# Loads of the first experts' weights cut in halves, and the table of slot weights built behind the first down product

## The chip, the cores and the metric

The kernel runs on 1 core of one Trainium2 chip. The metric is the device time of one execution in microseconds (us). Every expert weight is read from device memory once per execution.

## The reference

Two layers, each a mixer (eight heads of softmax attention with a forgetting bias, four heads of retention, an output projection) and then a mixture of 32 experts on 512 tokens of width 1024, two experts chosen for each token. All arithmetic is float32.

```python
for layer in range(2):
    x = x + mixer(rmsnorm(x, norm_mix_w[layer]), w_in[layer], fox_forget_b[layer], w_out[layer])
    x = x + hierarchical_moe(rmsnorm(x, norm_ffn_w[layer]), ...)
return rmsnorm(x, norm_final_w)

def hierarchical_moe(h, ...):
    # a softmax over 4 groups picks the group, top 2 of its 8 experts are taken, weights = group * pair
    ...
    def expert_block(args):
        xblk, e = args
        a = jax.nn.silu(xblk @ w_expert_gate[e]) * (xblk @ w_expert_up[e])
        return a @ w_expert_down[e]
    ...
    out = jax.ops.segment_sum(yb * w_buf[:, None], tok_buf, num_segments=N)
```

Gate and up are 1024 x 512 and down is 512 x 1024 for each expert, so each of the three is 2 MiB (2.10 MB) and an expert is 6.29 MB.

## The kernel before

**A layer** is a written-out list of steps for the mixer, the output projection, the router and the dispatch tables, and then a loop over the 32 experts. The list ends with the output projection ("wo"): for each of four token tiles and each half of the columns, eight chunks `c` of the contraction, three matmuls a chunk (L1715 to L1717). The second column half of tile 3 is the last; between its matmuls stand transposes, router logits and the ranks of chosen tokens. Then come four gathers by matmul of the first two experts' tokens (L1756), and the loop over experts.

**An expert** has 64 slots. TensorE does for expert `e`: gate (32 matmuls of 64 x 256, L1834) and up (32 more), then transposes of the hidden rows (L1843), for the middle experts the input transposes of the next expert (L1800), then down (16 matmuls, L1850). The result of expert `e - 1` is added to the tokens by one-hot matmuls, the "spread" (L1808): tiles 0 and 1 after gate and up of `e`, tiles 2 and 3 after its down. ScalarE makes the silu (L1016) and the scaled high part of the result (L1020). VectorE makes the product of gate and up (L1429), copies the transposed hidden rows (L1451), prepares the next input (L1415, L1426), the one-hot of the slots (L1438), the low part of the result (L1433), and adds the spread to the residual (L1170).

**The first experts** carry work for the tables besides. In expert 0 TensorE makes behind gate and up the table of tokens by slot (`slots_by_expert`, L1535) and the table of slot weights (`weights_by_expert`, L1542, eight float32 products that the profile counts as 16), then the transposes, then down. VectorE reads the token table (L1086, L1087), makes the product, copies the table of slot weights (`slot_weights`, L1102), which ScalarE's scaling waits for, copies the hidden rows, takes the input of expert 1, makes the one-hot, and then runs `further` (L1183 to L1207, 20 small operations for the tokens beyond 64 of an expert); only after that comes the low part of expert 0's result (L1433), for which the spread in expert 1 waits. `further` also gives the one-hots for a table that TensorE makes behind gate and up of expert 1 (L1535), and a weight table behind those of expert 2 (L1542).

**The loads** of expert weights are issued by SyncE (the SP queue), in order, into a ring of three expert-sized places. Each place is also used by the mixer: what is not yet read bars the load. So the order is: up of 0 after the last input projection; gate, up and down of 1 after the retention; gate of 0 and gate of 2 when the first column half of the output projection is done; down of 0, up of 2 and down of 2 when the second is done. From then on `load_expert` waits for gate, up and down of expert `e - 3` one after the other (semaphores `s_gh`, `s_gu`, `s_yf`) and loads the same matrix of `e` each time. GpSimd stores the normalized rows of each token tile (4 stores of 512 KB a layer) and gathers the rows of experts 2 and up with indirect DMAs (L760), through its own queue.

`down_rows` gives each of the 128 partitions two pieces of two rows each (8 KB each), and gate and up give it 8 consecutive rows, 16 KB.

Of the kernel before, what the change touches and what calls it, by code (L numbers as in the profile page):

```python
# [14 lines left out]
P = 128  # L15
DEPTH, T, D = 2, 512, 1024
NT = T // P
KC = D // P
# [4 lines left out]
NE = NG * EPG  # L23
# [3 lines left out]
NEG = -3.0e38  # L27

SLOTS = 64
N_SMALL = 6 * DEPTH + 2 * (DEPTH - 1)  # L30

MAXBLK = T // SLOTS
NOV = max(k for k in range(NE * MAXBLK)
# [7 lines left out]
EXPERT = 2 * KC * DE + (DE // P) * D  # L41
RING = 3
TAIL = NE % RING or RING
SLAB = KC * P
HT0 = 0
KT0 = HT0 + 2 * KC * T
# [252 lines left out]
def trunk_kernel(nc, x, norm_mix_w, w_in, fox_forget_b, w_out, norm_ffn_w, w_router_group, b_router_group,  # L299
                 w_router_expert, b_router_expert, w_expert_gate, w_expert_up, w_expert_down, norm_final_w,  # L300
                 const, rope, decay, number, out):
    with ExitStack() as ctx:
# [3 lines left out]
        def sem(name):  # L306
            return ctx.enter_context(nc.semaphore(name))
# [138 lines left out]
        s_tokn = sem("token_numbers_loaded")  # L446
# [111 lines left out]
        def _(sp):  # L558
# [42 lines left out]
            def down_rows(layer, e):  # L601

                return w_expert_down[layer, bass.ds(e, 1), :, :].rearrange("a (b p j) n -> p (a b) (j n)", b=2, p=P)

            def load_rows(layer, e, slot, i):

                weight = (w_expert_gate, w_expert_up)[i]
                sp.dma_start(wexp[slot][0][:, i, :, :].rearrange("p c n -> p (c n)"),
                             weight[layer, e, :, :].rearrange("(p c) n -> p (c n)", p=P)).then_inc(s_w[slot][i], 16)
# [3 lines left out]
                    load_rows(layer, e, slot, i)  # L613

            def load_down(layer, e, slot):
                sp.dma_start(wexp[slot][1].rearrange("p (b j) n -> p b (j n)", b=2), down_rows(layer, e)
                             ).then_inc(s_w[slot][2], 16)

            for layer in range(DEPTH):
                if layer == 0:  # L620
                    load_x(0)
                    load_slab(layer, 0)
                    load_x(2)
                    load_slab(layer, 1)
                    sp.dma_start(kst[:, P:NCONST], const[:, P:NCONST]).then_inc(s_const, 16)
                    sp.dma_start(tokn[:, :], number).then_inc(s_tokn, 16)
                load_slab(layer, RAW)
                if layer > 0:
                    sp.wait_ge(s_yf, layer * NE)
# [29 lines left out]
                load_rows(layer, 2, 2, 0)  # L659


                is_full(sp, ("wo", 3, 1), layer)
                load_down(layer, 0, 0)
                load_rows(layer, 2, 2, 1)
                load_down(layer, 2, 2)

                def load_expert(e, slot):

                    for i, used in enumerate((s_gh, s_gu)):
                        sp.wait_ge(used, e + (layer * NE - RING + 1))  # L670
                        load_rows(layer, e, slot, i)
                    sp.wait_ge(s_yf, e + (layer * NE - RING + 1))
                    load_down(layer, e, slot)

                for e in range(RING, NE):
                    load_expert(e, e % RING)
# [377 lines left out]
        def _(dve):  # L1054
# [154 lines left out]
            for layer in range(DEPTH):  # L1209
# [230 lines left out]
                def hidden(e):  # L1440
                    g = layer * NE + e + 1
                    if e == NE - 1:
                        for t in range(2):
                            add_spread(layer, e - 1, t)
                    dve.wait_ge(s_sg, g)
                    dve.wait_ge(s_gu, g)
                    gated_product().then_inc(s_h, 1)
                    if e == 0:
                        slot_weights(layer)
                    dve.wait_ge(s_hxf, g)  # L1450
                    nc.vector.tensor_copy(at(HX0, 256), bank[2][:, 0:256]).then_inc(s_hx, 1)  # L1451
                    if e < NE - 1:
                        take_input(e + 1)
                    if e == 0:
                        is_taken(dve, ("table",), layer)
                    slot_one_hot(e, slot_tok[:, e:e + 1]).then_inc(s_oh, 1)
                    if e == 0:
                        further(layer)
                    if e and e < NE - 1:
                        for t in range(2):  # L1460
                            add_spread(layer, e - 1, t)
# [12 lines left out]
                take_input(0)  # L1474
                route(layer)
                if layer == 0:
                    dve.wait_ge(s_tokn, 16)
# [47 lines left out]
        def _(pe):  # L1525
# [50 lines left out]
            for layer in range(DEPTH):  # L1576
                srow = layer * FH * NT
                for s in STEPS_OF[layer]:
# [126 lines left out]
                    elif kind in ("begin", "wp", "wo"):  # L1705
# [3 lines left out]
                        for c in chunks[kind] if kind != "wp" else range(2 * s[3], 2 * s[3] + 2):  # L1709
                            if t == 0:  # L1710
                                pe.wait_ge(s_ml, layer * KC + c + 1)
                                pe.wait_ge(s_wol, layer * KC + 4 * half + c // 2 + 1)
                            m_hi, m_lo = (m[:, c, P * t:P * (t + 1)] for m in (mix_hi, mix_lo))
                            w_h, w_l = wo_hi[half][:, c, :], wo_lo[half][:, c, :]
                            mm(o[:, :], m_hi, w_h, start=(c == 0), stop=False)  # L1715
                            mm(o[:, :], m_hi, w_l, start=False, stop=False)  # L1716
                            last = mm(o[:, :], m_lo, w_h, start=False, stop=(c == KC - 1))  # L1717
                    elif kind == "fT":
                        t, half = s[1], s[2]
                        is_taken(pe, ("wo", t, half), layer)  # L1720
# [103 lines left out]
                def gate_up(slot, before=None, parts=False):  # L1824

                    w = wexp[slot][0]
                    for i in range(2):
                        if before is not None:
                            before(i)
                        for c in range(KC):  # L1830
                            if parts and i == 0 and c == 4:
                                pe.wait_ge(s_xt, input_part(layer, 0))
                            for half in range(2):
                                last = mm(bank[i][SLOTS * half:SLOTS * (half + 1), 0:256],  # L1834
                                          xT[:, c % 4, c // 4, :], w[:, i, c, 256 * half:256 * (half + 1)],
                                          start=(c == 0), stop=(c == KC - 1))
                        if before is not None and i == 0:
                            last.then_inc(s_gh, 1)
                    return last
# [6 lines left out]
                def down(slot, into=3):  # L1846
# [7 lines left out]
                def per(i):  # L1854
                    return len(range(i, NE, RING))

                def expert(e):
                    i, g = e % RING, layer * NE + e + 1
                    loads = 16 * (layer * per(i) + e // RING + 1)
                    pe.wait_ge(s_xt, input_part(layer, e) - (e == 0))  # L1860

                    def ahead(part):
                        if part and e == NE - 1:
                            spread_block(e - 1, (0, 1))
                        pe.wait_ge(s_w[i][part], loads)

                    gate_up(i, ahead, e == 0).then_inc(s_gu, 1)
# [16 lines left out]
                    pe.wait_ge(s_w[i][2], loads)  # L1884
                    down(i).then_inc(s_yf, 1)
                    if e and e < NE - 1:
                        spread_block(e - 1, (2, 3))

                first_transpose()
                for e in range(NE):  # L1890
                    if e == 1:
                        for name in (("count",), ("table",), ("wtab",)):
                            is_taken(pe, name, layer)
                        may_fill(pe, ("more",), layer)
                    expert(e)

                o = ov[layer]
# [60 lines left out]
```

## Time and profile before

| | |
|---|---|
| time, median of 3 executions | 1526.78 us (1525.1 to 1527.63) |
| the profiled execution's own time | 1525.63 us |
| its span, first to last instruction | 1523.8 us |
| TensorE matmul busy | 1478.5 us (97%) |
| VectorE / ScalarE / GpSimd busy | 829.1 / 369.7 / 259.7 us |
| mean granted TensorE clock | 0.996 of full |
| DMA moved, mean | 463.84 MB, 304 GB/s |
| loop over experts, layer 0 | about 299.5 to 757 us |
| loop over experts, layer 1 | about 1050 to 1510 us |

Times of rows are us from the span's start. A matmul's busy time overlaps that of the next one, so the starts say more than the busy sums. The time from a DMA's issue to its landing contains the time that it stands behind earlier DMAs of its queue.

### The profile page before, as it was taken

Reading aid. Unit: us, or ns where it says so; the run is one execution under the profiler, and the core shown is the slowest. Engines: PE = TensorE matmul, PEld = TensorE weight load, DVE = VectorE, ACT = ScalarE, POOL = GpSimd, SP = SyncE. Lnnn points to the kernel's source line nnn. Section 1 sums busy time; section 2 is a strip of 40 time slices with the busy share of each in tenths; the row PEclk is TensorE's granted clock in tenths of the full one; section 3 lists DMA queues with packets and bytes.
Section 4 is the critical chain, followed back from the end, with each engine's and each line's share of the span. In section 5 each row is a group of like instructions: output and inputs, shape, how many; then the busy total and the mean of one; then the engine's idle time right before and its main releaser. Section 6 shows DMA issues by size and latency. Waiting matters only on the chain.

```text
span 1523.8 us, 23589 instructions
## 1 busy us (share of the span) xinstructions
PE 1478.5 (97%) x9360; PEld 929.8 (61%) x9360; DVE 829.1 (54%) x1602; ACT 369.7 (24%) x726; POOL 259.7 (17%) x155
## 2 busy tenths in 40 slices
PE   8999999999999999989999999999999999999996
PEld 6877768655555555545588777685555555554453
DVE  2267763655555455454525686636555545554546
ACT  6335464400000000000163354732000000000002
POOL 3342332110000000000134331401000000000001
PEclk9999999999999999999999999999999999999998
DMA  6442146599999999999833321478999999999995
GB/s 220 93 98 69 42 166 275 226 417 420 424 421 425 420 424 422 424 422 425 328 111 84 85 69 28 172 289 321 416 422 421 425 422 421 422 425 422 424 424 213
DMA packets 105616, 463.84 MB, mean 304 GB/s; under 512 B 16515, under 2 KB 59779, under 8 KB 72481
## 3 DMA queue, kind: packets, MB, share of 16 engines
q1 hardware_dynamic: 98208, 449.14, 73.7%
q0 software_dynamic: 5952, 12.09, 2.1%
q8 instruction: 78, 1.28, 0.3%
q10 hardware_dynamic: 1344, 1.05, 0.2%
q14 instruction: 34, 0.27, 0.1%
HBM read 463.81 MB, written 6.29 MB: 308 GB/s over the span
## 4 chain that ended last, share of the span: by engine, by line
PE 80%; DMA 17%; DVE 2%; issue 1%; DVEq 0%; ACTq 0%
PE bank L1834 23%; DMA area<-in_w_expert_up_dram 16%; PE bank L1850 11%; PE bank L1808 7%; PE bank L1645 5%; PE bank L1650 5%; PE bank L1649 5%; PE bank L1715 2%; PE bank L1717 2%; PE bank L1571 2%; PE bank L1716 2%; PE bank L1573 2%; PE bank L1572 2%; PE bank L1665 2%; PE bank L1687 1%; DVE area L1451 1%
## 5 line engine op out<-in xcount | busy, mean ns | idle before, releaser
L1834 PE MATMUL bank<-area 128*64 128x256 f32 x4096 | 459.8, 381 | 15.7 <-DMA area<-in_w_expert_up_dram 14.5
L1834 PEld LDWEIGHTS bank<-area 128*64 128x64 f32 x4096 | 287.5, 137 | 182.5 <-issue 24.3
L1170 DVE TENSOR_TENSOR xres<-xres,bank 128x512 f32<-128x512 f32 x512 | 316.2, 679 | 5.0 <-PE bank L1808 5.0
L1850 PE MATMUL bank<-area 128*64 128x512 f32 x1024 | 235.0, 601 | 7.5 <-DVE area L1451 2.2
L760 POOL DMA_INDIRECT area<-rows,gath x60 | 68.0, 1133 | 725.1 <-PE bank L1800 702.7
L1020 ACT ACTIVATE y_hi<-bank,slot_w 128x512 fp32r<-128x512 f32 x64 | 44.0, 688 | 580.3 <-PE bank L1850 580.3
L726 POOL TENSOR_TENSOR w_lo<-area,w_hi 128x1024 fp32r<-128x1024 f32 x55 | 135.2, 2459 | 272.7 <-ACT w_hi L833 272.6
L1429 DVE TENSOR_TENSOR area<-area,bank 128x256 f32<-128x256 f32 x64 | 26.9, 421 | 280.8 <-PE bank L1834 280.8
L1850 PEld LDWEIGHTS bank<-area 128*64 128x64 f32 x1024 | 68.3, 137 | 133.2 <-issue 110.4
L1645 PE MATMUL bank<-h_hi,w_hi 128*128 128x512 f32 x336 | 135.0, 402 | 0.0
L1650 PE MATMUL bank<-h_hi,w_lo 128*128 128x512 f32 x320 | 124.9, 390 | 0.0
L1649 PE MATMUL bank<-h_lo,w_hi 128*128 128x512 f32 x320 | 124.7, 390 | 0.0
L1808 PE MATMUL bank<-y_hi,onehot 64*128 64x512 f32 x512 | 115.1, 444 | 3.4 <-DVE xres L1170 1.7
L1808 PE MATMUL bank<-y_lo,onehot 64*128 64x512 f32 x512 | 102.2, 393 | 0.0
L1808 PEld LDWEIGHTS bank<-y_hi,onehot 64*128 64x128 f32 x512 | 48.2, 184 | 83.6 <-issue 75.9
L1016 ACT ACTIVATE area<-bank 128x256 f32<-128x256 f32 x64 | 24.5, 384 | 255.3 <-PE bank L1834 255.3
L1433 DVE SCALAR_TENSOR_TENSOR y_lo<-bank,slot_w,y_hi 128x512 fp32r<-128x512 f32 x64 | 48.1, 751 | 63.6 <-ACT y_hi L1020 63.5
L833 ACT ACTIVATE w_hi<-area 128x1024 fp32r<-128x1024 f32 x58 | 61.6, 1063 | 79.6 <-PE bank L1573 33.2
L1645 PEld LDWEIGHTS bank<-h_hi,w_hi 128*128 128x128 f32 x336 | 63.0, 187 | 22.9 <-issue 10.3
L1650 PEld LDWEIGHTS bank<-h_hi,w_lo 128*128 128x128 f32 x320 | 60.1, 188 | 13.1
L1649 PEld LDWEIGHTS bank<-h_lo,w_hi 128*128 128x128 f32 x320 | 60.1, 188 | 11.5
L1451 DVE COPY area<-bank 128x256 f32<-128x256 f32 x64 | 27.2, 425 | 67.4 <-PE bank L1843 67.1
(207 smaller groups left out, 1719.4 us busy)
## 6 DMA issues: line engine op xcount, KB each, us to landing
area<-in_w_expert_up_dram SPq DMA_DIRECT2D x64, 2048.0 KB, 26.3
area<-in_w_expert_gate_dram SPq DMA_DIRECT2D x64, 2048.0 KB, 25.4
area<-in_w_expert_down_dram SPq DMA_DIRECT2D x64, 2048.0 KB, 25.6
area<-in_w_in_dram SPq DMA_DIRECT2D x58, 512.0 KB, 3.9
area<-in_w_out_dram SPq DMA_DIRECT2D x4, 2048.0 KB, 11.2
rows<-area POOLq DMA_DIRECT2D x8, 512.0 KB, 3.2
area<-in_decay_dram SPq DMA_DIRECT2D x2, 1024.0 KB, 6.3
out_dram<-area SPq DMA_DIRECT2D x4, 512.0 KB, 2.9
```

The lines of the kernel that those rows point to most:

```text
L726: nc.gpsimd.tensor_tensor(w_lo[g % CUT][:, :, :], slab[g % RAW], w_hi[g % CUT][:, :, :].bitcast(F32), ALU.subtract).then_inc(s_wlo, 1)
L760: pool.indirect_dma_start(out=xg[e % 3], out_offset=None, in_=rows_dram, in_offset=bass.IndirectOffsetOnAxis(ap=gath[:, e:e + 1], axis=0), ...
L833: nc.scalar.activation(w_hi[g % CUT][:, :, :], slab[g % RAW], ACT.Copy).then_inc(s_whi, 1)
L1020: nc.scalar.activation(y_hi[e % 2][:, :], bank[3][:, :], ACT.Copy, scale=slot_w[:, e:e + 1]).then_inc(s_yh, 1)
L1170: tt(xs, xs, bank[4 + i][:, :], ALU.add).then_inc(s_sa[i], 1)
L1433: return nc.vector.scalar_tensor_tensor(out=y_lo[e % 2][:, :], in0=bank[found][:, :], scalar=weight, in1=y_hi[e % 2][:, :].bitcast(F32), o ...
L1645: mm(o[:, :], hi[:, c, :], h_hi[:, c, :], start=(c == 0), stop=False)
L1649: mm(o[:, :], hi[:, c, :], h_lo[:, c, :], start=False, stop=False)
L1650: last = mm(o[:, :], lo[:, c, :], h_hi[:, c, :], start=False, stop=(c == KC - 1))
L1808: yield mm(bank[4 + 2 * (t % 2) + half][:, :], onehot[parity][rows, P * t:P * (t + 1)], part[rows, :], start=(w_ == 0), stop=(w_ == 1))
L1834: last = mm(bank[i][SLOTS * half:SLOTS * (half + 1), 0:256], xT[:, c % 4, c // 4, :], w[:, i, c, 256 * half:256 * (half + 1)], start=(c == ...
L1850: last = mm(bank[into][SLOTS * half:SLOTS * (half + 1), :], hx[:, c % 2, c // 2, :], w[:, c, 512 * half:512 * (half + 1)], start=(c == 0), ...
```

## The change

- Some loads go in two halves, each with its own issue. Of the loads behind the second column half of the output projection (down of 0, up of 2, down of 2) the first halves no longer wait for its end, but for a new semaphore `s_part`, which TensorE raises at the end of chunk 3 of 8. Gate, up and down of expert 3 and gate of expert 4 go in halves as well: the first when half of the matmuls on the same matrix of the expert three before are done, the second as before.
- TensorE makes the table of slot weights behind down of expert 0, in front of gate of expert 1, and no longer between the token table and the transposes. On VectorE `slot_weights` moves behind the hidden rows and the input of expert 1, in front of the one-hot and `further`.
- TensorE's waits for three small tables being read move from before gate of expert 1 to behind its up.
- The load of the token numbers counts on the semaphore of the small loads, and its own semaphore goes.

```diff
+PART_OF = {(0, 0): 2, (0, 1): 3, (0, 2): 4, (1, 0): 5}
+HALVED = {(0, 2), (2, 1), (2, 2), (3, 0), (3, 1), (3, 2), (4, 0)}
...
-                is_full(sp, ("wo", 3, 1), layer)
-                load_down(layer, 0, 0)
-                load_rows(layer, 2, 2, 1)
-                load_down(layer, 2, 2)
+                for part in range(2):
+                    if part:
+                        is_full(sp, ("wo", 3, 1), layer)
+                    else:
+                        sp.wait_ge(s_part, PARTS * layer + 1)
+                    load_down_half(layer, 0, 0, part)
+                    load_rows_half(layer, 2, 2, 1, part)
+                    load_down_half(layer, 2, 2, part)
...
                     for i, used in enumerate((s_gh, s_gu)):
+                        if (e - RING, i) in PART_OF:
+                            sp.wait_ge(s_part, PARTS * layer + PART_OF[e - RING, i])
+                            load_rows_half(layer, e, slot, i, 0)
+                            sp.wait_ge(used, e + (layer * NE - RING + 1))
+                            load_rows_half(layer, e, slot, i, 1)
+                            continue
...
                     gated_product().then_inc(s_h, 1)
-                    if e == 0:
-                        slot_weights(layer)
                     dve.wait_ge(s_hxf, g)
                     nc.vector.tensor_copy(at(HX0, 256), bank[2][:, 0:256]).then_inc(s_hx, 1)
                     if e < NE - 1:
                         take_input(e + 1)
                     if e == 0:
+                        slot_weights(layer)
                         is_taken(dve, ("table",), layer)
...
+                            if (t, half, c) == (NT - 1, 1, KC // 2 - 1):
+                                last.then_inc(s_part, 1)
...
+                            if c == KC // 2 - 1 and (e, i) in PART_OF:
+                                last.then_inc(s_part, 1)
...
+                        if c == 1 and (e, 2) in PART_OF:
+                            last.then_inc(s_part, 1)
...
                     if e == 0:
                         slots_by_expert()
-                        weights_by_expert()
                     if e == 1:
+                        for name in (("count",), ("table",), ("wtab",)):
+                            is_taken(pe, name, layer)
+                        may_fill(pe, ("more",), layer)
                         pe.wait_ge(s_morein, layer + 1)
                         table(more_bank, hot_more, NMORE)
...
-                    down(i).then_inc(s_yf, 1)
+                    down(i, e=e).then_inc(s_yf, 1)
+                    if e == 0:
+                        weights_by_expert()
```

## Rows read from the trace of the kernel before

**Rows 1.** Chain of work that ended last: shares of the span by engine.
```profile
PE 80%; DMA 17%; DVE 2%; issue 1%; DVEq 0%; ACTq 0%
```

**Rows 2.** TensorE's waits in three stretches: 595 to 760, 1340 on, 300 to 595.
```profile
PE bank L1834 <- DMA area<-in_w_expert_up_dram: 6.5, 7, 1.5
...
PE bank L1834 <- DMA area<-in_w_expert_up_dram: 8.0, 8, 1.7
...
PE bank L1850 <- DVE area L1451: 0.7, 1, 0.7
```

**Rows 3.** Issues on SyncE's queue in order of time: start, duration, what.
```profile
285.74 0.38 SPq L616 DMA_DIRECT2D area<-in_w_expert_down_dram  x1
...
343.36 0.38 SPq L616 DMA_DIRECT2D area<-in_w_expert_down_dram  x1
...
592.81 0.38 SPq L616 DMA_DIRECT2D area<-in_w_expert_down_dram  x1
...
1036.36 0.38 SPq L616 DMA_DIRECT2D area<-in_w_expert_down_dram  x1
...
1095.19 0.38 SPq L616 DMA_DIRECT2D area<-in_w_expert_down_dram  x1
```

**Rows 4.** Issue to landing, last number, us; issues at 238.55, 286.67, 314.06.
```profile
area<-in_w_expert_gate_dram SPq DMA_DIRECT2D x1, 2048.0 KB, 7.6
...
area<-in_w_expert_down_dram SPq DMA_DIRECT2D x1, 2048.0 KB, 19.7
...
area<-in_w_expert_down_dram SPq DMA_DIRECT2D x1, 2048.0 KB, 8.6
```

**Rows 5.** The same for the down loads issued at 343.36, 592.81, 1036.36 and 1095.19.
```profile
area<-in_w_expert_down_dram SPq DMA_DIRECT2D x1, 2048.0 KB, 10.1
...
area<-in_w_expert_down_dram SPq DMA_DIRECT2D x1, 2048.0 KB, 36.5
...
area<-in_w_expert_down_dram SPq DMA_DIRECT2D x1, 2048.0 KB, 7.4
...
area<-in_w_expert_down_dram SPq DMA_DIRECT2D x1, 2048.0 KB, 11.0
```

**Rows 6.** TensorE in order of time, layer 0: start, busy, what, idle before.
```profile
281.45 0.39 PE L1717 MATMUL bank<-wo_hi,mix_lo 128*128 128x512 f32 x1
...
299.53 7.13 PE L1834 MATMUL bank<-area 128*64 128x256 f32 x64
...
307.50 1.95 PE L1542 MATMUL bank<-area,hot_slot 128*128 128x32 f32 x16
309.29 0.41 PE L1843 MATMUL bank<-kst,area 128*128 128x128 f32 x2
310.37 3.65 PE L1850 MATMUL bank<-area 128*64 128x512 f32 x16 [0.67 <-DVE area L1451]
...
321.85 0.50 PE L1808 MATMUL bank<-y_hi,onehot 64*128 64x512 f32 x2
```

**Rows 7.** TensorE in order of time, layer 1.
```profile
1032.01 0.40 PE L1717 MATMUL bank<-wo_hi,mix_lo 128*128 128x512 f32 x1
...
1061.01 4.84 PE L1850 MATMUL bank<-area 128*64 128x512 f32 x16 [0.52 <-DVE area L1451]
```

**Rows 8.** VectorE in order of time, expert 0 of layer 0.
```profile
308.06 0.41 DVE L1429 TENSOR_TENSOR area<-area,bank 128x256 f32<-128x256 f32 x1
309.56 0.19 DVE L1102 COPY slot_w<-bank 128x32 f32<-128x32 f32 x1 [1.09 <-PE bank L1542]
...
311.35 0.49 DVE L1438 TENSOR_SCALAR onehot<-tokn,slot_tok 128x512 fp32r<-128x512 int16 x1 [0.25 <-DVE area L1415]
...
319.16 0.75 DVE L1433 SCALAR_TENSOR_TENSOR y_lo<-bank,slot_w,y_hi 128x512 fp32r<-128x512 f32 x1
```

**Rows 9.** Stretches: length, busy time by engine, granted clock, DMA share, GB/s.
```profile
280.00:285.00 5.00, 5.00 (x31) 4.37 (x29) 3.74 (x17) 3.21 (x5) 0.72 (x1) 1.00 0.03 10
...
1061.00:1062.00 1.00, 0.99 (x4) 0.38 (x6) 0.72 (x3) 0.00 (x0) 0.96 (x1) 0.50 0.96 410
```

More of the change, by code:

```diff
@@ L29 @@
 SLOTS = 64
-N_SMALL = 6 * DEPTH + 2 * (DEPTH - 1)
+N_SMALL = 6 * DEPTH + 2 * (DEPTH - 1) + 1
 MAXBLK = T // SLOTS
@@ L43 @@
 TAIL = NE % RING or RING
+PART_OF = {(0, 0): 2, (0, 1): 3, (0, 2): 4, (1, 0): 5}
+PARTS = 1 + len(PART_OF)
+HALVED = {(0, 2), (2, 1), (2, 2), (3, 0), (3, 1), (3, 2), (4, 0)}
 SLAB = KC * P
@@ L445, in trunk_kernel @@
         s_const, s_small = sem("const_loaded"), sem("small_loaded")
-        s_tokn = sem("token_numbers_loaded")
+        s_part = sem("first_half_of_weights_used")
         s_first = sem("first_layer_small_loaded")
@@ L603, in down_rows, with load_rows_half, load_down_half @@
                 return w_expert_down[layer, bass.ds(e, 1), :, :].rearrange("a (b p j) n -> p (a b) (j n)", b=2, p=P)
+            def load_rows_half(layer, e, slot, i, part):
+                weight = (w_expert_gate, w_expert_up)[i]
+                cs = slice(KC // 2 * part, KC // 2 * (part + 1))
+                sp.dma_start(wexp[slot][0][:, i, cs, :].rearrange("p c n -> p (c n)"),
+                             weight[layer, e, :, :].rearrange("(p c) n -> p c n", p=P)[:, cs, :]
+                             .rearrange("p c n -> p (c n)")).then_inc(s_w[slot][i], 16)
+            def load_down_half(layer, e, slot, part):
+                sp.dma_start(wexp[slot][1].rearrange("p (b j) n -> p b (j n)", b=2)[:, part, :],
+                             down_rows(layer, e)[:, part, :]).then_inc(s_w[slot][2], 16)
             def load_rows(layer, e, slot, i):
+                if (e, i) in HALVED:
+                    for part in range(2):
+                        load_rows_half(layer, e, slot, i, part)
+                    return
                 weight = (w_expert_gate, w_expert_up)[i]
@@ L615, in load_down @@
             def load_down(layer, e, slot):
+                if (e, 2) in HALVED:
+                    for part in range(2):
+                        load_down_half(layer, e, slot, part)
+                    return
                 sp.dma_start(wexp[slot][1].rearrange("p (b j) n -> p b (j n)", b=2), down_rows(layer, e)
@@ L625, in _ @@
                     sp.dma_start(kst[:, P:NCONST], const[:, P:NCONST]).then_inc(s_const, 16)
[L626 removed]
+                    sp.dma_start(tokn[:, :], number).then_inc(s_small, 16)
                 load_slab(layer, RAW)
@@ L659, in _ @@
                 load_rows(layer, 2, 2, 0)
-                is_full(sp, ("wo", 3, 1), layer)
-                load_down(layer, 0, 0)
-                load_rows(layer, 2, 2, 1)
-                load_down(layer, 2, 2)
+                for part in range(2):
+                    if part:
[5 more added lines that the diff above has]
+                    load_down_half(layer, 2, 2, part)
                 def load_expert(e, slot):
                     for i, used in enumerate((s_gh, s_gu)):
+                        if (e - RING, i) in PART_OF:
[4 more added lines that the diff above has]
+                            continue
                         sp.wait_ge(used, e + (layer * NE - RING + 1))
                         load_rows(layer, e, slot, i)
-                    sp.wait_ge(s_yf, e + (layer * NE - RING + 1))
-                    load_down(layer, e, slot)
+                    if (e - RING, 2) in PART_OF:
+                        sp.wait_ge(s_part, PARTS * layer + PART_OF[e - RING, 2])
+                        load_down_half(layer, e, slot, 0)
+                        sp.wait_ge(s_yf, e + (layer * NE - RING + 1))
+                        load_down_half(layer, e, slot, 1)
+                    else:
+                        sp.wait_ge(s_yf, e + (layer * NE - RING + 1))
+                        load_down(layer, e, slot)
                 for e in range(RING, NE):
@@ L1476, in _ @@
                 if layer == 0:
-                    dve.wait_ge(s_tokn, 16)
+                    dve.wait_ge(s_small, 16 * N_SMALL)
                 for e in range(NE - 1):
@@ L1822, in spread_block, with gate_up @@
                             made[2 + half].then_inc(s_sf[2 * (t % 2) + half], 1)
-                def gate_up(slot, before=None, parts=False):
+                def gate_up(slot, before=None, parts=False, e=None):
                     w = wexp[slot][0]
@@ L1844, in hidden_transpose, with down @@
                     return last
-                def down(slot, into=3):
+                def down(slot, into=3, e=None):
                     w = wexp[slot][1]
@@ L1851, in down, with loaded, pieces @@
                                       w[:, c, 512 * half:512 * (half + 1)], start=(c == 0), stop=(c == 3))
-                    return last
-                def per(i):
-                    return len(range(i, NE, RING))
+                        if c == 1 and (e, 2) in PART_OF:
+                            last.then_inc(s_part, 1)
+                    return last
+                def loaded(layer, e, n):
+                    def pieces(upto):
+                        return sum(1 + ((x, n) in HALVED and x < NE - 2) for x in range(e % RING, upto, RING))
+                    return 16 * (layer * pieces(NE) + pieces(e + 1))
                 def expert(e):
                     i, g = e % RING, layer * NE + e + 1
-                    loads = 16 * (layer * per(i) + e // RING + 1)
                     pe.wait_ge(s_xt, input_part(layer, e) - (e == 0))
@@ L1864, in ahead @@
                             spread_block(e - 1, (0, 1))
-                        pe.wait_ge(s_w[i][part], loads)
-                    gate_up(i, ahead, e == 0).then_inc(s_gu, 1)
+                        pe.wait_ge(s_w[i][part], loaded(layer, e, part))
+                    gate_up(i, ahead, e == 0, e).then_inc(s_gu, 1)
                     if e == 0:
                         slots_by_expert()
-                        weights_by_expert()
                     if e == 1:
+                        for name in (("count",), ("table",), ("wtab",)):
+                            is_taken(pe, name, layer)
+                        may_fill(pe, ("more",), layer)
                         pe.wait_ge(s_morein, layer + 1)
@@ L1883, in expert @@
                     pe.wait_ge(s_hx, g)
-                    pe.wait_ge(s_w[i][2], loads)
-                    down(i).then_inc(s_yf, 1)
+                    pe.wait_ge(s_w[i][2], loaded(layer, e, 2))
+                    down(i, e=e).then_inc(s_yf, 1)
+                    if e == 0:
+                        weights_by_expert()
                     if e and e < NE - 1:
@@ L1890, in _ @@
                 for e in range(NE):
[L1891 to L1894, printed above, removed]
                     expert(e)
```

## The prediction

> **What bounds the kernel now.** I read the chain of work first. It names TensorE for 80% and DMA for 17% [rows 1], which looks like a TensorE-bound kernel. The waits of TensorE by stretch correct that. From 300 to 595 us it waits for no load at all, only 0.7 us for VectorE; from 595 on it waits in nearly every expert for the up weights, 6.5 us in all, and in layer 1's last stretch 8.0 us [rows 2]. So each layer's loop has two regimes: TensorE paces its first two thirds, the loads its last third, and the loop ends when the last load has landed. The issue and landing times show why. From the down load issued at 343.36 to the one issued at 592.81, which are 18 experts apart, issues come every (592.81 - 343.36) / 18 = 13.86 us [rows 3], which is TensorE's pace. Landings go from 343.36 + 10.1 = 353.46 to 592.81 + 36.5 = 629.31 [rows 3, 5], every 15.33 us. The queue therefore grows by 1.47 us an expert until the ring of three is full. The reader is to see that TensorE time in the early experts can be spent freely, as long as the load queue does not run empty; and that a load which is issued earlier helps only until the queue meets the pace at which places come free.
>
> That last point sets the size of everything. An idle queue lands such a load in 7.4 us [rows 5] (7.6 for a gate [rows 4]). The down load at 343.36, of expert 5, took 10.1, the one of expert 5 in layer 1, issued at 1095.19, took 11.0 [rows 5]. So the queue ahead of them was only 10.1 - 7.4 = 2.7 us and 11.0 - 7.4 = 3.6 us long. Whatever is won at the start of the loads, no more than this passes expert 5; beyond it the queue is empty and the load waits for its place. Later loads have more queue ahead, so this is the narrow point. An earlier one, down of 3 issued at 314.06, took 8.6 [rows 4], but it is itself issued earlier, and in halves, by the change.
>
> **The change part by part.**
>
> *First halves behind the output projection.* The end of chunk 3 is the end of the matmul at 281.45, so 281.84, against an issue at 285.74 now [rows 3, 6]: 3.9 us earlier. In layer 1 it is 1032.41 against 1036.36, 3.95 us [rows 3, 7]. The DMA engines are idle there (share 0.03, 10 GB/s from 280 to 285 [rows 9]), so the head start is real. It costs SyncE three more issues of about 0.4 us, with nothing else queued behind them that is due.
>
> *Pieces of experts 3 and 4.* With the head start, down of 2 lands at 286.67 + 19.7 - 3.9 = 302.5 instead of 306.4 [rows 4]. The first half of gate of 3 is free when a quarter of gate and up of expert 0 is done, 299.53 + 1.8 = 301.3 [rows 6]. Half a load is half of 15.33 / 3, 2.55 us, so from an idle queue it lands in 7.6 - 2.55 = 5.05 us, at 306.4; without a hole it would be 305.0. The hole eats 1.4 of the 3.9 us; about 2.5 us of head start goes on. Without the halves the hole would be 1.8 us longer, since the whole of gate waits for a second quarter. Up and down of 3 and gate of 4 in halves keep the queue from emptying again until down of 4. I carry 2.5 us, in layer 1 too.
>
> *Cost of cutting.* Seven loads a layer become fourteen. In a standing queue the three loads of an expert and a gather take 15.33 us for 6.29 MB, which is 410 GB/s, as much as a microsecond of full DMA share shows (410 GB/s [rows 9]), so a load in a queue has hardly any cost of its own; I take 0, with 7.4 - 5.1 = 2.3 us for each extra load as the upper bound, if none of its start overlapped. The row thus speaks for 0. The Trainium skill ("DMA: Bandwidth & Descriptors", Bandwidth, and Anatomy of one DMA) speaks against the change: about 2.0 us fixed for each DMA beside its bytes, and a 1 MiB transfer, which is what a half is, at 341 GB/s against 425 for 16 MB. Paid in full by that page, 14 more loads would be 28 us and the sum some 1553 us; the landing pitch above does not agree, since three loads an expert would then take over 20 us.
>
> *The table of slot weights on TensorE.* It stands from 307.50 to the transposes at 309.29, so 1.8 us [rows 6]. It is partly cover: VectorE's product ends only at 308.06 + 0.41 = 308.47 [rows 8], so the transposes can start at 308.5, 0.8 us earlier and not 1.8. Down then starts at 309.6 instead of 310.37 and ends at 313.25; the table behind it ends at 315.05. Gate of expert 1 starts 1.0 us later than now (310.37 + 3.65 = 314.02 [rows 6]).
>
> *The same table on VectorE.* This is where the stall goes. Its copy is at 309.56 now, and the one-hot, all 20 operations of `further` and then the low part of result 0 follow, from 311.35 to 319.16 + 0.75 = 319.91 [rows 8], so 8.56 us. TensorE needs that low part at 321.85 [rows 6], so now it is 1.9 us early. After the change the copy can't come before 315.1, the one-hot starts 0.35 us behind it, at 315.45, and the low part ends at 324.0. Expert 1's gate, up and small table would let the spread start at 321.85 + 1.0 = 322.85; it starts at 324.05. TensorE waits 1.2 us there, and from then on is 2.2 us late. The input of expert 1 is taken ahead of the table, and ScalarE's high part (0.7 us) is done well inside the 8.56. Product of expert 1 (0.42 us) follows the low part and is ready before its transposes. Nothing brings the 2.2 us back before the loads bind: it sits between 321.85 and 595, where no cover is to be used up. But the load issues move with it.
>
> *The moved waits for the tables and the changed semaphore* cost 0: they pass at once when TensorE comes to them, the last of them (slot weights read, 315.4) 6 us before up of expert 1 ends.
>
> **Sum.** The queue at expert 5 is 2.7 us in layer 0; issues come 2.2 us later, so the landing can be at most 2.7 - 2.2 = 0.5 us earlier, less than the 2.5 carried: 0.5. Layer 1: 3.6 - 2.2 = 1.4. TensorE's lateness is paid from its waits for loads, 6.5 and 8.0 us [rows 2], so the end follows the landings. Together 1.9 us. Against the profiled execution's 1525.63 us (span 1523.8, 1.8 around it) that is 1523.7; this execution lies 1.15 us under the median, so against the median it is 1524.9 us. A change of 0.2%, 3.05 us, is about what a measurement of this kernel can tell from none; this lies inside.
>
> **The rivals.**
>
> *The whole head start arrives.* It needs the stall at the spread to be missing, for instance with TensorE only 0 to 1 us late. Then layer 0 gives 2.5 or at most 2.7 and layer 1 2.5: 5.0 us, 1521.8. For it: the idle DMA share before 285. Against it: the order on VectorE, in which 8.56 us follow the copy; only 8.1 us of TensorE work stand against it.
>
> *The queue's floor is higher than 7.4.* Down of 3 took 8.6 with scarcely anything ahead [rows 4]. If an empty queue costs 8.6 in the midst of gathers, layer 0 gives 10.1 - 8.6 - 2.2 = -0.7 and layer 1 11.0 - 8.6 - 2.2 = +0.2, so 0.5 us slower, 1527.3. The head start is then wholly given back to late places.
>
> *The clock falls in the new waits (the case on the slower side).* In layer 1 the granted clock is 0.50 at 1061 [rows 9], the lower level of 1.2 GHz, right behind the small tables and transposes, and down of expert 0 takes 4.84 instead of 3.65 us [rows 6, 7], 1.2 more. The change makes two waits on TensorE, 0.9 us ahead of the transposes and 1.2 at the spread. A fall at each, in both layers, would add 1.2 us to down and up to 1.7 us to 3.4 us of gate work: TensorE 5.1 us late instead of 2.2. It decides once lateness exceeds the queue, 2.7 and 3.6: then every microsecond goes to the end. The price is 5.1 - 2.7 + 5.1 - 3.6 = 3.9 us, 1530.7. Slower by 0.2% needs 4.7 us a layer. The Trainium skill ("TensorE: Matmul & The Clock Gate", The HAM clock gate) has the throttled state as the default, which activity releases, so it too lets less activity cost clock; in layer 0 the same work without that wait kept full clock. In the other direction, were layer 1's fall to vanish, TensorE would be 1.2 less late and the gain 1.1 more.
>
> *The cut loads pay their start.* By the bound above up to 2.3 us each for 14 loads, 32 us; a tenth of that already makes the case a slower one. Against it stands the pitch of 15.33 us. The Trainium skill's rule on fixed cost (the same page and sections) is this rival's.
>
> *The change does not do what it says*: first halves issued no earlier. SyncE has nothing to wait for between the issue of gate of 2 and these, so I give it nothing of its own.
>
> **How the numbers follow.** The likeliest case, 1524.9 with its own range 1523 to 1526.5, gets 0.48 (0.07 faster, 0.41 same). The whole head start 0.16 (0.13 faster, 0.03 same). The higher floor 0.18 (same). The clock 0.09 (0.07 slower, 0.02 same). Paid starts 0.04 (slower). Other things 0.05 (0.02 slower, 0.03 same). That is 0.20 faster, 0.67 same, 0.13 slower. The range goes down to 1521.5, which holds the full head start, and up to 1528.5, past the higher floor and the measurement's own scatter (1525.1 to 1527.6 before); it leaves out most of the clock case and of the paid starts.
>
> **What the profile after would show.** Right: three first halves issued near 281.8 and 1032.4, DMA rate up before 285; down of expert 0 starting 0.8 us earlier (about 309.6), gate of expert 1 about 315.0, a wait of about 1.2 us for VectorE's `y_lo` before the spread at about 324; the landing of down of 5 close to 353 with 7.5 to 8 us from issue; TensorE's waits for loads in the last third down from 6.5 to some 4.8 us. Wrong: no wait before that spread; a landing of down of 5 over 2 us earlier; a granted clock of 0.5 in the first experts of both layers; a landing pitch above 15.33 us. The prediction falls if the queue at expert 5 is not the narrow point, or if the 8.56 us on VectorE shrink.

## The result, and the profile after

The changed kernel takes 1532.36 us (median of 5 executions, 1529.49 to 1534.17) against 1525.4 of the kernel before beside it: a ratio of 1.0036, with an interval of 1.0025 to 1.0047. It is slower, by some 5.5 us (3.8 to 7.2 by the interval; the two medians, of 5 executions each, lie 7.0 us apart). The forecast was 1524.9 in a range of 1521.5 to 1528.5.

The profiled execution is one of its two fastest: 1530.1 us, a span of 1528.2 against 1523.8. First TensorE's waits, 300 to 595, 595 to 765 and 1345 on. Each row is who waited for whom: us in total, times, longest.

```profile
PE bank L1849 <- DVE y_lo L1473: 1.1, 1, 1.1
PE bank L1886 <- DVE area L1469: 0.9, 1, 0.9
PE bank L1893 <- DVE area L1489: 0.5, 1, 0.5
...
PE bank L1875 <- DMA area<-in_w_expert_up_dram: 6.3, 7, 1.3
PE bank L1875 <- DMA area<-in_w_expert_gate_dram: 1.2, 1, 1.2
...
PE bank L1875 <- DMA area<-in_w_expert_up_dram: 6.4, 6, 1.5
```

Before, the 6.5 us for up in the second stretch [rows 2] had this line beside them:

```profile
PE bank L1834 <- DMA area<-in_w_expert_gate_dram: 1.0, 1, 1.0
```

The two new waits are there, 0.9 us ahead of the transposes and 1.1 ahead of the spread. What is missing is their payment: in layer 0 the waits for loads near the end are 6.3 + 1.2 = 7.5 us with the gate's, as much as before (6.5 + 1.0), not 1.7 less. In layer 1 a part was paid: the up waits fell from 8.0 to 6.4 us, all waits for loads from 8.6 to 7.2.

TensorE and VectorE in experts 0 and 1 of layer 0, in order of time:

```profile
300.66 7.13 PE L1875 MATMUL bank<-area 128*64 128x256 f32 x64
307.71 1.07 PE L1574 MATMUL bank<-hot_exp,hot_slot 128*128 128x32 f32 x8
309.65 0.44 PE L1886 MATMUL bank<-kst,area 128*128 128x128 f32 x2 [0.87 <-DVE area L1469]
310.60 3.65 PE L1893 MATMUL bank<-area 128*64 128x512 f32 x16 [0.52 <-DVE area L1489]
314.19 1.97 PE L1581 MATMUL bank<-area,hot_slot 128*128 128x32 f32 x16
316.09 7.13 PE L1875 MATMUL bank<-area 128*64 128x256 f32 x64
...
325.32 0.50 PE L1849 MATMUL bank<-y_hi,onehot 64*128 64x512 f32 x2 [1.11 <-DVE y_lo L1473]
```

```profile
316.27 0.19 DVE L1142 COPY slot_w<-bank 128x32 f32<-128x32 f32 x1 [4.93 <-PE bank L1581]
316.61 0.48 DVE L1478 TENSOR_SCALAR onehot<-tokn,slot_tok 128x512 fp32r<-128x512 int16 x1
...
324.42 0.75 DVE L1473 SCALAR_TENSOR_TENSOR y_lo<-bank,slot_w,y_hi 128x512 fp32r<-128x512 f32 x1
```

Counted from expert 0's gate, down starts at 9.94 us (10.84 before), the spread at 24.66 (22.32 before) [rows 6]: 2.3 us late, as forecast. The whole profile starts expert 0 some 1.1 us later (300.66 against 299.53); kernels that differ from the one before only behind this point start it between 300.0 and 301.0, so that is taken as scatter of executions, and times below are counted from expert 0.

Now the loads. Windows with the same distances from expert 0's start: the 16 us before it and 2 behind, the next 3, then 25 to 65, then 65 to 285. The last three numbers are granted clock, DMA share and GB/s. The kernel before:

```profile
283.50:301.50 18.00, 16.79 (x79) 10.00 (x79) 12.63 (x48) 5.65 (x10) 3.54 (x5) 1.00 0.90 347
301.50:304.50 3.00, 3.00 (x30) 2.01 (x28) 2.11 (x9) 0.39 (x1) 0.00 (x0) 1.00 1.18 422
324.50:364.50 40.00, 39.84 (x302) 22.58 (x300) 21.21 (x40) 3.21 (x6) 3.42 (x3) 1.00 1.00 421
364.50:584.50 220.00, 218.71 (x1618) 119.75 (x1616) 119.26 (x208) 17.14 (x32) 18.27 (x16) 1.00 1.01 423
```

The changed kernel:

```profile
284.70:302.70 18.00, 16.79 (x81) 9.97 (x81) 12.62 (x48) 5.65 (x10) 3.55 (x5) 1.00 0.98 398
302.70:305.70 3.00, 3.00 (x32) 1.99 (x30) 2.04 (x8) 0.39 (x1) 0.00 (x0) 1.00 0.73 218
325.70:365.70 40.00, 39.76 (x296) 22.38 (x294) 22.25 (x41) 3.13 (x6) 3.42 (x3) 1.00 0.99 393
365.70:585.70 220.00, 218.71 (x1620) 119.74 (x1618) 118.76 (x208) 16.89 (x32) 18.31 (x16) 1.00 1.01 423
```

These are the bytes of layer 0. The halves move (398 - 347) x 18 us = 0.92 MB more before the loop, worth 2.2 us at 423 GB/s. In the next 3 us the queue is dry and 0.61 MB, 1.4 us, are given back. From 25 to 65 us, the loads of experts 4 to 6, another (421 - 393) x 40 = 1.12 MB, 2.6 us, are lost; TensorE frees the places 2.3 us later, and late_at_1 below shows that this alone takes bytes from this stretch. The 20 us between, from 5 to 25, differ little (406 GB/s before, 402 after), and from 65 us on both run at 423 GB/s. Together some 0.8 to 0.9 MB are missing, 1.9 to 2.1 us, and the loop of layer 0 is 2.3 us longer. The loop of layer 1 is 1.2 us longer; with the 1.1 us of the start that is the 4.4 us between the two spans, within 0.2.

### The profile page after: what moved, and what is told of

It reads as the page before. It is cut to its first block, busy times and chain, and to the rows that moved or that the text cites. A ratio compares the mean times of both kernels' runs of the same rounds, so it can differ in the third digit from the quotient of the medians.

```text
span 1528.2 us, 23603 instructions
## 1 busy us (share of the span) xinstructions
PE 1480.3 (97%) x9360; PEld 931.4 (61%) x9360; DVE 830.2 (54%) x1602; ACT 370.3 (24%) x726; POOL 259.7 (17%) x155
## 4 chain that ended last, share of the span: by engine, by line
PE 82%; DMA 14%; DVE 3%; issue 1%; DVEq 0%; ACTq 0%
PE bank L1875 23%; DMA area<-in_w_expert_up_dram 14%; PE bank L1893 12%; PE bank L1849 7%; PE bank L1684 5%; PE bank L1689 5%; PE bank L1688 5%; PE bank L1754 2%; PE bank L1756 2%; PE bank L1610 2%; PE bank L1755 2%; PE bank L1612 2%; PE bank L1611 2%; PE bank L1704 2%; PE bank L1726 1%; DVE area L1489 1%
```

## The experiments

Each is timed in 5 rounds against the kernel before on the same chip. "Falls" are stretches at the lower level of the granted clock.

**1. The halves alone.** The table goes back behind the token table, on VectorE behind the product.

```diff
                         slots_by_expert()
+                        weights_by_expert()
...
-                    if e == 0:
-                        weights_by_expert()
```

> The early halves stay, the table of slot weights goes back between the token table and the transposes. Theory A (the moved table is the cost: it makes TensorE 2.3 us late a layer, and that lateness passes to the end whole because the load queue near expert 6 has no room): no lateness, so the time is at or under the kernel before, 1521 to 1525.5. If the queue has no room in the other direction either, the head start brings nothing and it is 1525.4. Theory B (the cut loads cost something of their own): as slow as the whole change, 1530 to 1533.

Measured: 1525.74 us, 0.9993 (0.9984 to 1.0002). The cut is no loss, and hardly a gain. The same stretches in its trace:

```profile
284.30:302.30 18.00, 16.79 (x81) 9.96 (x81) 12.60 (x48) 5.66 (x10) 3.54 (x5) 1.00 0.98 399
302.30:305.30 3.00, 3.00 (x31) 1.99 (x28) 2.07 (x9) 0.38 (x1) 0.00 (x0) 1.00 0.69 205
325.30:365.30 40.00, 39.84 (x302) 22.58 (x300) 21.16 (x40) 3.21 (x6) 3.42 (x3) 1.00 1.01 419
```

0.94 MB won, 0.65 MB lost in the hole, and hardly anything later (0.08 MB): 0.2 to 0.3 MB, 0.5 to 0.7 us in layer 0, is what remains of 3.8 us of earlier issue.

**2. The table alone.** `PART_OF` and `HALVED` empty, the three loads whole behind the output projection.

> All loads whole and at their old places, only the table of slot weights is moved, on TensorE and on VectorE. Theory A: the whole loss is here, 1529 to 1533, with a wait of about 1.1 us for y_lo in expert 1. Theory B: 1525 to 1527, lateness hidden by the load waits at the end.

Measured: 1533.06 us, 1.0042 (1.0029 to 1.0055). The whole loss is here.

**3. Cut, but issued at the old time.** The halves of experiment 1 with `PART_OF = {}` and the first issues behind `is_full(sp, ("wo", 3, 1), layer)`.

> The same loads cut in two as in the change, but both halves issued at the old moment, one behind the other; the table at its old place. Theory A: cutting is free, 1525 to 1526.5. Theory B: the cut alone costs, 1527 or more (2 us for each of the 14 further loads would be 1553).

Measured: 1526.8 us, 0.9996 (0.9987 to 1.0004). Cutting is free to within the measurement; theory B falls.

**4. Low part first.** On VectorE `further(layer)` moves behind `result_low(0)`.

> The whole change, but on VectorE the low part of result 0 stands ahead of the 20 operations for further tokens. Theory A: the wait of 1.1 us before the spread goes and one of about 0.6 us for the small table of expert 1 comes, so TensorE is about 1.7 us late instead of 2.3 and the time 1.0 to 1.5 us under the whole change. Theory B: no difference to the whole change.

Measured: 1531.27 us, 1.0020 (1.0012 to 1.0029). The wait went as expected from 1.1 us for `y_lo` to one for the small table, 0.6 us long:

```profile
326.16 1.03 PE L1574 MATMUL bank<-hot_more,hot_slot 128*128 128x16 f32 x8 [0.61 <-DVE hot_more L1242]
```

That is some 3.1 us over the kernel before, where the whole change is 5.5 to 6.0 over: a larger gain than the 1.0 to 1.5 us expected, though the intervals just touch.

**5 to 7. Lateness by itself, at three places.** Filler in the kernel before, nothing else changed; the line is for expert 1, then 12, then 5.

```diff
+                    if e == 1:
+                        unread(2, 256, 256, 256, 256, 256)
```

> The kernel before with five filler products of 256 columns (some 2.3 us of TensorE, results unread) behind gate and up of expert 1, in each layer. Nothing else moves. Theory A (lateness of TensorE in the first experts passes to the end whole, since the load queue has no room there): 4 to 5 us over the kernel before, 1531 to 1532.5. Theory C (the queue has 2.7 and 3.6 us of room at expert 5, and what the moved table cost beyond that came from the clock alone; the filler keeps TensorE busy): at most 0.5 us over.

> The same filler behind gate and up of expert 12 instead of 1, where loads take some 20 us from issue to landing. Theory A: the queue has room here and the lateness is paid from the waits for loads near the end: 0 to 0.5 us over the kernel before. Theory D (the end is set by TensorE's own work after all, and any lateness counts wherever it is): 4 to 5 us over.

> The kernel before with the same filler of 2.3 us behind gate and up of expert 5 in each layer. It delays the places for experts 8 and later. Theory A (the load queue stands on its floor up to the loads of expert 6 and grows by about 1.4 us an expert behind them): by the loads of expert 8 it has 2.9 us of room, so the lateness is free: 0 to 1 us over the kernel before. Theory E (the room is nil everywhere in the first half of the loop): 4 us over, as at expert 1.

Measured: at expert 1 1531.46 us, 1.0025 (1.0015 to 1.0034); at expert 5 1527.22, 0.9997 (0.9988 to 1.0006); at expert 12 1526.92, 0.9999 (0.9990 to 1.0008). The same 2.3 us of TensorE work cost some 3.8 us for both layers at expert 1 (2.3 to 5.2 by the interval), and nothing that can be told from zero at 5 or 12. Theories C, D and E fall. The waits for loads in the last third show the payment itself. Layer 0 of late_at_12 (late_at_5 has the same two lines):

```profile
PE bank L1834 <- DMA area<-in_w_expert_up_dram: 5.0, 5, 1.5
PE bank L1850 <- DMA area<-in_w_expert_down_dram: 0.2, 1, 0.2
```

That is 5.2 us instead of 7.5: the 2.3 us are paid there. In late_at_1 all waits for loads of layer 0 are still 7.5 us: nothing was paid. The 25 to 65 us window of late_at_1, then of late_at_12:

```profile
326.00:366.00 40.00, 39.76 (x286) 22.35 (x286) 21.84 (x41) 2.84 (x5) 3.42 (x3) 1.00 0.99 400
```

```profile
326.00:366.00 40.00, 39.76 (x296) 22.47 (x296) 22.27 (x41) 3.22 (x6) 3.42 (x3) 1.00 1.00 421
```

**8. The tables for further tokens later.** The two tables of experts 1 and 2 are made in experts 12 and 13 of the kernel before, and VectorE reads them in expert 14 instead of 3; **9.** the same on top of the halves alone.

```diff
-                    if e == 1:
+                    if e == 12:
                         pe.wait_ge(s_morein, layer + 1)
                         table(more_bank, hot_more, NMORE)
-                    if e == 2:
+                    if e == 13:
                         weight_table(more_bank[:, NMORE:2 * NMORE], hot_more_w
```

> The kernel before, with the two tables for further tokens made in experts 12 and 13 instead of 1 and 2 (1.0 and 1.9 us of TensorE a layer), and VectorE's reading of them moved from expert 3 to 14. Theory A: earliness in the first experts passes to the end as lateness does, up to 2.9 us a layer, so 3 to 5.8 us under the kernel before, 1521.5 to 1524.5. Theory D: no difference, since the same work is done.

> The same move of the two tables, with the early halves of the loads kept and the table of slot weights at its old place. Theory A: the head start of the halves and the places that come free earlier add up, 5 to 8 us under the kernel before, 1519 to 1522. Theory D: as the halves alone, about 1 us under.

Measured: 1526.48 us, 0.9995 (0.9986 to 1.0005), and with the halves 1525.29, 0.9984 (0.9975 to 0.9993). Theory A missed here: being 2.9 us early brings nothing by itself. In the kernel before, the loads already run at 421 GB/s from 25 us on, which suggests that only more bytes at the start can help. Number 9 has the lowest ratio of the study, some 2.4 us under the kernel before, but less than half of what theory A expected of it; its interval overlaps those of numbers 1 and 8.

**10, 11. Deeper halves.** `PART_OF` holds experts 0 to 5 in full, so that the loads of experts 3 to 8 go in halves: on number 1, then on number 9.

> The early halves, with the table of slot weights at its old place, and the loads of experts 3 to 8 all cut, the first half issued when half of the matmuls on its place are done (18 pieces a layer instead of 4). Theory A: places at the narrow point, the loads of experts 5 and 6, come free 1.8 us earlier, so the head start reaches the end: 2 to 4 us under the kernel before, 1523 to 1525. Theory F (the floor there is the loads' own transfer and start, not the moment a place comes free): as the shallow halves, about 1 us under.

> The same deep halves with the two tables for further tokens in experts 12 and 13. Theory A: both free the narrow point, only the head start is left as a limit: 3 to 5 us under the kernel before, 1522 to 1524. Theory F: as with the shallow halves, 2.4 us under.

Measured: 1526.19 us, 0.9989 (0.9980 to 0.9998), and 1525.44, 0.9989 (0.9979 to 0.9998). Not told apart from the shallow halves, as theory F expected; the reason that theory F gives is not tested by itself.

**12. Filler in the new waits of the whole change.**

```diff
                         slots_by_expert()
+                        is_taken(pe, ("count",), layer)
+                        unread(2, 128, 128, 128)
...
+                    if e == 1:
+                        unread(2, 128, 128, 128, 128)
```

> The whole change with filler products in the two new waits of TensorE (three of 128 columns behind the token table of expert 0, four in front of the spread in expert 1; some 0.7 and 0.9 us, results unread), so that it does the same work with hardly any idle time there. Theory A (lateness alone): as the whole change, 1530.5 to 1532.5. Theory G (the clock falls because of the new waits, and that is part of the cost): 1 to 2 us under the whole change, with a granted clock of 1.00 in experts 0 and 1.

Measured: 1529.19 us, 1.0009 (1.0000 to 1.0018), with a mean granted clock of 0.996 in all 11 executions. TensorE is exactly as late as in the whole change (the spread at 325.29), but the ratio is 1.0009 where the whole change has 1.0036 and, in number 13, 1.0039: some 4 us less, more than expected, with intervals that do not meet. So part of the cost was the clock: theory G.

**13. The whole change again.** No edit.

> The whole change once more, unedited, so that it stands beside the next three on the same chip. Theory A with G (lateness of 2.3 us a layer passes to the end, and the rest is falls of the clock in experts 0 and 1): 1531 to 1532.5, with a mean granted clock spread from 0.993 to 0.996. Theory A alone: the same time as with filler in the new waits, 1529 to 1530.

Measured: 1533.1 us, 1.0039 (1.0025 to 1.0053), clock 0.993 to 0.995. Its profile caught four falls, here the windows around them:

```profile
311.00:314.00 3.00, 2.75 (x9) 0.83 (x10) 0.95 (x3) 0.00 (x0) 2.39 (x3) 0.67 1.02 429
329.00:332.00 3.00, 3.00 (x12) 1.44 (x12) 2.28 (x5) 0.00 (x0) 1.04 (x1) 0.51 1.03 393
1067.00:1070.00 3.00, 3.00 (x10) 0.76 (x8) 0.39 (x1) 0.00 (x0) 2.22 (x3) 0.54 1.02 429
1083.00:1086.00 3.00, 3.00 (x16) 1.99 (x18) 0.53 (x3) 0.00 (x0) 0.00 (x0) 0.57 1.03 355
```

and what they do to the two down products of layer 0, behind the two new waits:

```profile
310.30 0.44 PE L1886 MATMUL bank<-kst,area 128*128 128x128 f32 x2 [0.87 <-DVE area L1469]
311.25 5.35 PE L1893 MATMUL bank<-area 128*64 128x512 f32 x16 [0.52 <-DVE area L1489]
...
327.68 0.50 PE L1849 MATMUL bank<-y_hi,onehot 64*128 64x512 f32 x2 [1.13 <-DVE y_lo L1473]
...
330.04 4.85 PE L1893 MATMUL bank<-area 128*64 128x512 f32 x16
```

5.35 and 4.85 us instead of 3.65, and the 25 to 65 us window moves 367 GB/s:

```profile
326.30:366.30 40.00, 38.71 (x269) 21.29 (x270) 21.60 (x43) 2.84 (x5) 3.42 (x3) 0.96 0.94 367
```

**14 to 16. Filler where the kernel before waits anyway**, on the kernel before, on number 1 and on number 9.

```diff
                         unread(0, 512, 512)
+                    if s == ("rank", NT - 1):
+                        unread(0, 256, 256)
...
                     hidden_transpose().then_inc(s_hxf, 1)
+                    if e == 0:
+                        is_taken(pe, ("table",), layer)
+                        unread(4, 128, 128)
```

> The kernel before, with filler products in two waits that it has anyway (two of 256 columns in the wait for the one-hots of tile 3, two of 128 columns behind the transposes of expert 0), results unread, nothing late by them. Theory G: the kernel before pays for falls of the clock too; 1525 to 1526, clock 0.996 in nearly every execution, and some 4 us under the whole change with filler (1529.2), which is then the price of the lateness alone. Theory A without G: no difference to the kernel before.

> Early halves, the table of slot weights at its old place, and the same filler. Theory G: the gain of the halves shows without the falls, 1 to 2 us under the kernel before with filler. Theory F (the head start ends at the floor of the queue): within 0.5 us of it.

> Early halves, the two tables for further tokens in experts 12 and 13, and the same filler. Theory A with G: the fastest of all, 1521.5 to 1524. Without G: as without filler, 1525.

Measured: 1526.95 us, 1.0003 (0.9994 to 1.0012); 1525.64, 0.9992 (0.9983 to 1.0001); 1524.85, 0.9989 (0.9981 to 0.9998). The expectation failed: the clock still falls in experts 0 of both layers (0.66 in 310 to 315 and 1060 to 1065 of before_filled), so these say nothing against or for theory G.

**What ties them together.** Start of gate of expert 3 and of expert 31, us behind expert 0's, from each trace:

| kernel | layer 0: 3, 31 | layer 1: 3, 31 |
|---|---|---|
| tables_late | 42.0, 442.5 | 42.0, 442.3 |
| halves_only | 44.9, 440.6 | 46.5, 443.1 |
| cut_in_place | 44.9, 441.8 | 44.9, 442.5 |
| before | 44.9, 442.0 | 46.0, 444.4 |
| kept_busy | 47.2, 443.7 | 47.2, 444.4 |
| the change | 47.2, 444.3 | 48.8, 445.6 |
| late_at_1 | 48.8, 445.7 | 48.8, 446.5 |
| the change again | 50.4, 447.0 | 50.1, 447.9 |

From 42.0 to 44.9 the end does not move. From 44.9 on, 5.2 to 5.5 us later at expert 3 (the change again against before and cut_in_place) is 5.0 to 5.4 us later at expert 31. Lateness that is already there at expert 3 counts nearly in full, whether work, a wait or the clock made it. Each row is one execution, and single ones stray by 1 us and more: halves_only ends layer 0 1.2 us before cut_in_place from the same start, and the change in layer 1 is 2.8 us behind the kernel before at expert 3 and 1.2 at expert 31.

## Why the prediction was wrong

**Right in mechanism and size** are the terms ahead of the queue. The first halves issue 3.8 us ahead of the second (282.99 against the end of the projection at 286.83). Down of expert 0 starts 0.9 us earlier (0.8 forecast), gate of expert 1 1.1 later (1.0), the wait for `y_lo` is 1.1 us (1.2) and the lateness 2.3 us (2.2). Cutting costs nothing. The hole behind down of 2 costs 1.4 to 1.5 us (1.4).

**The step that failed** is the room: "The queue at expert 5 is 2.7 us in layer 0; issues come 2.2 us later, so the landing can be at most 2.7 - 2.2 = 0.5 us earlier". Down of expert 5 landed at 346.81 + 9.4 = 356.21, so 55.5 us behind expert 0 instead of 53.9: 1.6 later, and by the window from 25 to 65 us 1.12 MB were missing. There was next to no room: 2.3 us of lateness made the loops 1.9 us longer (kept_busy, worked out below), so 0 to 0.5 us in place of 2.7 and 3.6. I had measured room as time to landing above that of a single load in an idle queue. But the loads ahead of it in the queue wait for places of the same late engine and come later too. That they take their part of the queue with them is my reading, which no run isolates. The row that should have warned was down of 3, which took 8.6 us [rows 4]: the queue had just been almost dry there, and I set it aside as issued earlier and in halves. The rival built on it, the higher floor, gave 1527.3: the right direction, with a room that was still too large. Of the two thirds of the loop that I called free of charge, experts 0 and 1 are not; late_at_5 and late_at_12 show that experts 5 and 12 are, and no run says where between 1 and 5 it turns.

**A second size**: the 3.8 us of earlier issue was 2.2 us of bytes, and 0.5 to 0.7 behind the hole, where I carried 2.5. With the lateness of 2.3 there was nothing to set against it.

**The rival on the slower side** was given 0.09, and it was part of what happened. The second profile of the change has its picture, a fall behind each of the two new waits, in both layers, with TensorE 5.5 us late in layer 0 where the rival said 5.1; the first profile has one fall in the loops, at the same place as the kernel before, at down of expert 0 in layer 1. I had taken layer 0 of the one trace as proof that the clock holds there, though both layers do the same work with a short wait ahead of down, 0.67 and 0.52 us [rows 6, 7]. But late_at_5 and late_at_12, which differ from the kernel before only later, have a fall in expert 0 in both layers.

**The cost of cutting** was rightly put at nothing. The Trainium skill ("DMA: Bandwidth & Descriptors", Anatomy of one DMA, and Bandwidth) gives the 2.0 us and the 341 GB/s for DMAs that GpSimd issues; these loads are issued by SyncE, and cut_in_place at 0.9996 shows no such cost.

**The sum as it stands.** Lateness of 2.3 us without falls makes the loops 1.9 and 1.9 us longer (kept_busy against cut_in_place: 443.7 - 441.8 = 1.9 and 444.4 - 442.5 = 1.9), so some 3.8 us. That fits late_at_1, 3.8. These are single executions, and kept_busy has the early halves as well, which cut_in_place has not, so the lateness alone may have cost up to 0.7 us a layer more. The whole change costs 5.5 to 6.0, kept_busy beside the kernel before only 1.4, and its profile has no fall in the loops while the kernel before has some. So I estimate some 4 us of falls in the whole change's executions (5.5 to 6.0, less 1.4) and some 2.4 us in the kernel before (3.8 less 1.4). The shares are settled only to about 1.5 us, half the width of the intervals. Why landings suggest more room than the bytes show is not settled either; that a landing is the last of 16 engines and the others run dry sooner would explain it, but nothing here tests it.

## What to carry to other kernels

When loads wait for places that the compute engine frees, room in the queue is not a load's time to landing less that of an idle one: look for the last point at which the queue was dry, and count all lateness behind it in full until the queue has grown again. Compare bytes moved in windows that start at the same event; a head start shows at once how much of it survives the next hole. And work that fills an engine's unavoidable wait costs little where it stands: moving it out puts it on the path and leaves a wait behind which the clock can fall.

## What the runs showed of the hardware

An idle wait of 0.87 us on TensorE behind narrow products was followed by a fall of the granted clock in some executions (down of expert 0 5.35 us instead of 3.65) and not in others (3.65 in the first profile of the same kernel), while with three filler products of 128 columns in it (0.91 us) and four in the other new wait the mean clock was 0.996 in 11 of 11 executions. The fall also came in expert 0 of kernels without that wait (late_at_5, late_at_12), so the wait is not needed for a fall. That it makes falls more frequent rests on kept_busy and on the mean clocks, 0.9936 to 0.9946 on average for the change and 0.9950 to 0.9956 for the kernel before. Two loads of 1 MiB cost no more than one of 2 MiB in a standing queue (0.9996, 0.9987 to 1.0004, for 14 loads cut), and from idle a 1 MiB half landed 4.9 us after its issue against 7.4 for a whole load. The executions of one kernel spread over 3 to 6 us, and part of it goes with the mean clock, 0.993 to 0.997: those of the kernel before average 1528.6 us at 0.993 and 1526.1 at 0.997, but kept_busy spreads over 3.7 us with one value of the clock, 0.996.
